# Differential attention: the head norm in three sets of tokens, spread over the next key projection, and two output projections begun inside the last head norm

## The reference, cut to what matters

```python
def _diff_attend(q, k, v, lam):
    s = jnp.einsum('bqhte,bkhte->bhtqk', q, k).astype(jnp.float32) * (q.shape[-1] ** -0.5)
    p = jax.nn.softmax(s, axis=-1)
    a = (p[:, :, 0] - lam * p[:, :, 1]).astype(v.dtype)
    return jnp.einsum('bhqk,bkhe->bqhe', a, v)
...
    yb = _sweep_query_blocks(lambda n, qn: _diff_attend(qn, kb_all, vb_all, lam), qb)
    yb = rmsnorm(yb, b_subln_g) * (1.0 - lam_init)
    y = jnp.concatenate([ya.reshape(B, S, -1), yb.reshape(B, S, -1)], axis=-1) * jax.nn.silu(g)
    x = x + gate * (y @ w_out)
```

## Time and profile before

| | |
|---|---|
| runs | 3954.23, 3945.95, 3941.73 us; median 3945.95 us |
| span of the profiled execution (first to last instruction) | 3950.5 us; the profile gives no other time for this execution |
| mean granted TensorE clock | 0.942 of full speed |
| PE busy | 3589.2 us, 91% of the span |
| PEld busy | 2836.7 us, 72% |
| DVE busy | 1908.9 us, 48% |
| ACT busy | 1348.4 us, 34% |
| POOL busy | 237.2 us, 6% |
| differential attention, heads 0 to 3 | about 2310 to 2820 us, then the last head norm until 2838 us |

### The profile page before, as it was taken

The page is one execution under the profiler, slowest core; times in us unless marked ns, Lnnn a source line. Parts: engine busy times, 40 slices in busy tenths (PEclk is TensorE's granted clock), DMA queues, the critical chain, the costliest instruction groups (busy, mean ns, idle before and its releaser), DMA issues. The chain is left out here.

```text
span 3950.5 us, 44451 instructions
## 1 busy us (share of the span) xinstructions
PE 3589.2 (91%) x18426; PEld 2836.7 (72%) x18426; DVE 1908.9 (48%) x3579; ACT 1348.4 (34%) x2445; POOL 237.2 (6%) x342
## 2 busy tenths in 40 slices
PE   7999989997989999999999988888798998888888
PEld 5888867664777888888766577777686665676676
DVE  4599952443834323322566644445345444224443
ACT  3211253544212211111322334444324555324441
POOL 1011110000100000000000000000000000000000
PEclk9699998998999999999999998988798999889999
DMA  3223321000521111111201011000221000000112
GB/s 113 91 100 119 128 107 55 29 22 36 204 96 32 49 51 56 48 43 46 99 29 35 24 34 34 27 29 23 105 74 53 32 32 26 27 24 16 34 50 84
DMA packets 69289, 228.90 MB, mean 58 GB/s; under 512 B 8728, under 2 KB 12824, under 8 KB 69088
## 3 DMA queue, kind: packets, MB, share of 16 engines
q1 hardware_dynamic: 43056, 132.68, 10.2%
q0 software_dynamic: 22576, 80.80, 6.0%
q10 hardware_dynamic: 3456, 12.58, 0.8%
HBM read 179.37 MB, written 36.17 MB: 55 GB/s over the span
## 5 line engine op out<-in xcount | busy, mean ns | idle before, releaser
L2421 PE MATMUL PS<-m,m 128*128 128x512 f32 (+3 forms) x3560 | 1426.3, 402 | 96.0 <-DVE m L2767 18.8
L2423 PE MATMUL PS<-m,m 128*128 128x512 f32 (+3 forms) x3560 | 1368.5, 386 | 0.0
L2422 PE MATMUL PS<-m,m 128*128 128x512 f32 (+3 forms) x3560 | 1366.9, 385 | 0.0
L2421 PEld LDWEIGHTS PS<-m,m 128*128 128x128 f32 (+2 forms) x3560 | 681.1, 192 | 300.1 <-issue 43.6
L2423 PEld LDWEIGHTS PS<-m,m 128*128 128x128 f32 (+2 forms) x3560 | 681.3, 192 | 135.6 <-issue 1.6
L2422 PEld LDWEIGHTS PS<-m,m 128*128 128x128 f32 (+2 forms) x3560 | 684.7, 193 | 120.2 <-issue 2.3
L2767 DVE TENSOR_TENSOR m<-m,m 128x1024 fp32r<-128x1024 f32 (+5 forms) x204 | 210.7, 1033 | 423.9 <-ACT m L2609 422.9
L2701 ACT COPY m<-PS 128x512 f32<-128x512 f32 x352 | 205.4, 589 | 458.1 <-PE PS L2528 457.4
L2538 PE MATMUL PS<-m,m 128*64 128x256 f32 (+1 forms) x1408 | 310.4, 413 | 28.4 <-ACT m L2701 21.2
L2519 PE MATMUL PS<-m,m 64*128 64x256 f32 (+5 forms) x1968 | 253.6, 369 | 62.5 <-ACT m L2690 43.5
L2519 PEld LDWEIGHTS PS<-m,m 64*128 64x128 f32 (+1 forms) x1968 | 214.5, 198 | 111.3 <-ACT m L2690 54.3
(11 more groups left out here) (190 smaller groups left out, 3037.1 us busy)
## 6 DMA issues: line engine op xcount, KB each, us to landing
m<-in_w SPq DMA_DIRECT2D x220, 512.0 KB, 3.3
g_scratch<-m ACTq DMA_DIRECT2D x24, 512.0 KB, 2.6
m<-g_scratch POOLq DMA_DIRECT2D x24, 512.0 KB, 4.7
m<-in_w SPq DMA_DIRECT2D x32, 256.0 KB, 2.6
x_scratch<-m POOLq DMA_DIRECT2D x2, 4096.0 KB, 13.5
m<-m POOLq DMA_DIRECT2D x60, 128.0 KB, 2.7
m<-in_xT POOLq DMA_DIRECT2D x24, 256.0 KB, 7.8
y_scratch<-m POOLq DMA_DIRECT2D x12, 512.0 KB, 2.9
```

The costliest lines, as they stand in the source:

```text
L2421: pe.e.engine.matmul(o, L[0], X[0], start=start, stop=False)
L2422: pe.e.engine.matmul(o, L[0], X[1], start=False, stop=False)
L2423: return pe.e.engine.matmul(o, L[1], X[0], start=False, stop=stop)
```

## The change

- In heads 1 and 2 the order of the fill becomes: squares of the head norm, transposes of v, then the k projection with the rest of the head norm put between its sets of tokens, then q, then v. `cols` and `root` are done for each of the three sets of tokens by themselves (16, 16 and 8 single-column hardware matmuls), and their `rows` and `subln` follow one set of the k projection later. The weights of k are therefore loaded before those of q, for all heads.
- In head 3's fill the norm of head 2 stays in one piece, but it too goes by three sets.
- After head 3, seven k-steps of the first set of `eo0` and seven of `eo1` are put between the three sets of the last head norm; their eighth k-step (k = 7) follows once the result is split. `cols` and `rows` there take turns on banks 6 and 7.
- The counts given to `Fill` and `head` change from (87, 87, 87, 63) and (11, 11, 11, 11) to (79, 85, 85, 62) and (3, 24, 24, 10).

The diff:

```diff
-            tiles += [(f"f{s}{h + 1}", 8, 128) for s in "qkv"]
+            tiles += [(f"f{s}{h + 1}", 8, 128) for s in "kqv"]
...
+            if last and "settled" in u:
+                assert u["settled"]()
...
-        def next_steps(chunks, nxt, banks):
+        def next_steps(chunks, nxt, banks, free=()):
...
-                    e_ = copy_to(lambda t0, tn: z[:, t0:t0 + tn], scale)
+                    e_ = copy_to(lambda t0, tn: z[:, t0:t0 + tn], scale, after=free)
...
             def finish_steps(h, free, banks):
                 p.add("gsilu", n=h, z=zg[:, :], after=gate_done)
+                squared = []
                 for t0, tn in CH2:
-                    n = p.id()
-                    p.add("square", n=n, x=yt[:, t0:t0 + tn], q=zq[:, t0:t0 + tn], r=None, after=list(free))
+                    squared.append((S.square, p.id()))
+                    p.add("square", n=p.n, x=yt[:, t0:t0 + tn], q=zq[:, t0:t0 + tn], r=None, after=list(free))
                     yield
-                of = roots(take(banks), [[(zq[:, 128 * y:128 * y + 128], cc("o128")[:, 0:1]), (ident, squares[h % 2][:, y:y + 1])]
-                                         for y in range(10)], [(S.square, n), squares_done[h]], eps=False, at_=inverse)
+
+                def roots_of(c):
+                    t0, tn = CH2[c]
+                    return roots(take(banks), [[(zq[:, 128 * y:128 * y + 128], cc("o128")[:, 0:1]), (ident, squares[h % 2][:, y:y + 1])]
+                                               for y in range(t0 // 128, (t0 + tn) // 128)], [squared[c], squares_done[h]], eps=False,
+                                 at_=inverse[:, t0 // 128:(t0 + tn) // 128])
+                of = roots_of(0)
                 yield
                 for c, (t0, tn) in enumerate(CH2):
                     b = take(banks)
-                    r, t = spread(b, of, t0 // 128, tn)
+                    r, t = spread(b, of, 0, tn)
...
-                    yield
+                    if c < 2:
+                        of = roots_of(c + 1)
+                        yield
...
+                settled_heads.append(h)
+                yield
...
                 def steps():
+                    old = finish_steps(h - 1, ready, at.fill_banks) if h else iter(())
                     if h:
-                        yield from finish_steps(h - 1, ready, at.fill_banks)
+                        for _ in range(3):
+                            next(old)
+                            yield
+                    if h == 3:
+                        yield from old
                     yield from token_major_steps(zv, 10, [(vt, None, 0, 0, 128)], ev["v"], at.fill_banks, at.v_after)
                     if h < 3:
-                        qk, v = ({s: x for s, x in nxt.items() if s in of} for of in ("qk", "v"))
-                        yield from next_steps(CHE, qk, at.fill_banks)
+                        q, k, v = ({s: x for s, x in nxt.items() if s == of} for of in "qkv")
+                        if h:
+                            next(old)
+                        yield from weave(next_steps(CHE, k, at.fill_banks, list(begin + rest)), old, 8)
+                        yield from next_steps(CHE, q, at.fill_banks)
                         yield from weave(next_steps(CHE, v, at.fill_banks), rotate_steps(nxt, done), 2)
...
-                at.run(units, list(begin), Fill(steps(), 11 + (76 if h < 3 else 52)), 11, tail,
+                at.run(units, list(begin), Fill(steps(), (3, 9, 9, 10)[h] + (76 if h < 3 else 52)), (3, 24, 24, 10)[h], tail,
...
-            for _ in finish_steps(3, ready, None):
-                pass
+            eo_evac = {}
+            eo = [linear_steps(f"eo{d}", h_rhs, CH2[0:1] + CH2[2:3] + CH2[1:2], lambda *a, d=d: eo_evac[d](*a), ahead=2 - d)
+                  for d in range(2)]
+            old = finish_steps(3, ready, [6, 7])
+            for n, of in zip((0, 0, 0, 4, 3, 7), (0, 0, 0, 0, 0, 1)):
+                next(old)
+                for _ in range(n):
+                    next(eo[of])
+            finish(old)
...
+        for d in range(2):
+            eo_evac[d] = add_gated(d, sums)
+            finish(eo[d])
+            if d == 0:
+                w_prep(st["use"] + 1)
+        two_sets([(f"eo{d}", h_rhs, add_gated(d, sums)) for d in range(2, 8)], CH2[0:1] + CH2[2:3], CH2[1:2],
```

More of the change, by code:

```diff
@@ L2001, in schedule @@
             p.add("gain8", out=g8[:, :], g=vc("subln"))
-            stored, squares_done = [], {}
+            stored, squares_done, settled_heads = [], {}, []
             def load_steps():
@@ L2081, in schedule @@
                                   "keys": [(128 * y, vt[:, k0 // 128 + y, :]) for y in range(n // 128)],
+                                  "settled": lambda h=h: len(settled_heads) >= h,
                                   "evac": (yt[:, 128 * b0:128 * b0 + 256], slice(0, P), None, y_free)})
                 units[0]["hook"] = functools.partial(p.add, "ready", on="pe", after=list(rest))
-                at.run(units, list(begin), Fill(steps(), 11 + (76 if h < 3 else 52)), 11, tail,
+                at.run(units, list(begin), Fill(steps(), (3, 9, 9, 10)[h] + (76 if h < 3 else 52)), (3, 24, 24, 10)[h], tail,
                        Fill(gate_steps(f"eg{4 + h}", CH2, done, at.tail_banks), 24) if h < 3 else None)
@@ L2110, in schedule @@
         sums = Squares(bufs[1], bufs[0])
-        two_sets([(f"eo{d}", h_rhs, add_gated(d, sums)) for d in range(8)], CH2[0:1] + CH2[2:3], CH2[1:2],
+        for d in range(2):
[4 more added lines that the diff above has]
+        two_sets([(f"eo{d}", h_rhs, add_gated(d, sums)) for d in range(2, 8)], CH2[0:1] + CH2[2:3], CH2[1:2],
                    modulated("od", bufs, sums, [0, 2]))
```

## The result

The changed kernel takes 3970.58 us (median of 4 runs, 3964.43 to 3973.69), the one before 3946.40 (4 runs): ratio 1.0056, interval 1.0042 to 1.0070. It is slower by 24 us by the medians, by 22 by the ratio, and outside the range that was forecast.

What follows compares the result with a forecast made beforehand. TensorE was taken to bound the kernel, losing to waits and half clock in heads 1 and 2. Terms 2 × 1.1 + 0.9 − 1.5 + 2.4 = +4.0 us on 3945.95 gave about 3950 us, range 3936 to 3960.

Steps and rivals of the forecast that it cites:

- What comes: waits: Heads 1 and 2, each: new TensorE waits of 1.9, 0.7, 2.5 and 2.3, sum 7.4 us, 2.6 more than before.
- the sum for heads 1 and 2: Heads 1 and 2, each: +2.6 for waits − 1.5 for clock = +1.1 us, between about −4.5 and +5.
- the copy was waited for before too and is not counted: Heads 1 and 2: ScalarE's copy at each set's end, 0.7 us, left out because it was already waited for.
- What comes: clock: Heads 1 and 2, each: half-clock surcharge 4.3 us first, 1.7 in later groups; sum 6.0, 1.5 less than before.
- falls in every group: Rival, heads 1 and 2 and last norm: projections run at half clock, +6 us per head, about 3966 us; chance 0.11.
- Head 3's fill: Norm of head 2 in head 3's stage: more root and `subln` waits, 0.9 us later; bounds −1 and +3.
- Head 0's stage: Stage without a norm: smaller share per pair leaves fill for the last pairs, 1.5 us gained; bounds −3 and 0.
- The last norm: After head 3: +0.7 us from the exposed wait for the split, +2.4 with half clock; bounds −1 and +6.
- The loads of x cost nothing: After the last norm: x loads move 6 us later, costed at nothing, at most 2 us, as TensorE has six banks.
- The table drain: Rival, heads 1 and 2: first root 2.8 us later in each through drains at table switches, about 3955 us; chance 0.03.

Runs made afterwards that it cites:

- set ends last: Kernel before, with head 2's norm by sets in head 3's fill, and ten early steps, estimate 82, in heads 1 and 2: 3929.69 us, ratio 0.9945.
- that and the tail: "set ends last" plus last norm by sets, seven early steps of each output projection, third projection's weights ahead of the late addition: 3928.82 us, 0.9947 to kernel before.

## Why the prediction was wrong, step by step

- **What comes: waits** was right for what it looked at. Forecast 1.9, 0.7, 2.5 and 2 × 1.15; measured 1.78, 0.69, 2.53 (3.19 in head 2) and 2 × 1.10. The first pair of head 1 became 5.6 us shorter (22.7 to 17.1). The second became 14.6 us longer (9.9 to 24.5), with 21 more projection matmuls (45 instead of 24, 4.8 us at 0.23 each) and the rest of the norm in it.
- The step that failed is the sum for heads 1 and 2, +1.1 each, measured +11.6 and +11.1: it has no term for the waits in the later pairs. It stopped at the last step of the norm. For head 0 I did ask what a smaller share per pair does, for heads 1 and 2 not, although the 24 early steps and the estimate of 85 were in the diff. The order of the later pairs would have shown a set's copy right ahead of the exponentials in five of them: at 1.5 to 2.4 us each, 8.7 us of waits where there had been 2.9. And "the copy was waited for before too and is not counted" holds only as long as the copies keep their places.
- **What comes: clock.** First stretch 13.7 us (forecast 12 to 14), then 3.4 and 6.8 us; I had taken half of 3.4 us of surcharge for the later ones. (The 3.4 us are 17 projections at 0.2 us, which is one group; for both groups the upper end had to be 6.8.) The half-clock time came to 3.4 us more than before, where the forecast had less. All of the busy time that head 1 gained is 2.2 us, so the rival "falls in every group", whose time of 3966 us was the nearest, was near for the wrong reason: it asked for 6 us of clock per head.
- **Head 3's fill**: forecast +0.9, measured −5.3. Idle time fell by only 1.8 us (32.3 to 30.5); the rest is clock, 0.82 instead of 0.78, and unchanged code reached 0.83 once, so how much is the change's is open. I priced waits there and left the clock out, which moves this stage by more.
- **Head 0's stage**: forecast −1.5, measured 0.0: TensorE's idle time fell by 0.8 us and its busy time rose by as much.
- **The last norm**: forecast +2.4, measured +4.3. The wait for the split was right (3.85). That tail took +2.4 to +7.0 over unchanged code, by which profiles are compared. "The loads of x cost nothing" was wrong: I looked for TensorE's banks, not for what stands behind the late addition in the lists of ScalarE and VectorE. Putting that right gave 2.6 us.
- The table drain of about 1.4 us in the Trainium skill, "ScalarE: Activation LUTs", section "What ACT_TABLE_LOAD costs", was weighed and left out of the sum. After, the exponential behind a load that begins at 2426.64 starts at 2427.93, 1.29 us later, and the root wait came out at 2.53 us as computed without a drain. So the trace doesn't agree with that section:

```profile
2426.64 1.28 ACT L2723 ACT_TABLE_LOAD   x1
2426.67 3.48 PEld L2490 LDWEIGHTS PS<-m,m 128*128 128x128 f32 x16 [0.88 <-ACT m L2685]
2426.67 3.57 PE L2490 MATMUL PS<-m,m 128*128 128x1 f32 x16 [0.47 <-ACT m L2685]
2427.93 1.11 ACT L2723 ACTIVATE m<-PS,m 128x1024 f32<-128x1024 f32 x1
```

## What to carry to other kernels

When filler work is dealt out in equal shares, and a share is as long as its own period, its end falls on one place in every round; look where that is in each engine's list, put it behind the work that the next round waits for, and count again whenever an offset changes. On an engine with an in-order list, an instruction that waits for a late input stops what stands behind it on that engine, and on others that need that; so read both lists, not the busier one. And price a shift of filler over the whole stage, not only where the new work stands.

## What the runs showed that I had not expected

Two steps of a fill, 1.4 us of work, moved a stage of some 135 us by 10 to 13 us, in both orders. And head 0, with the same instructions in the same order, took 120.8 to 120.9 us in some profiles and 123.6 to 124.5 in seven others; in these TensorE was idle no longer but spent about 13 us at half clock instead of 3. Head 1 has the same code in "set ends last" and "that and the tail" and took 131.0 and 133.7 us, with 20.5 and 27.3 us at half clock. A gain of 3 or 4 us in a single stage of a single profile is therefore no evidence by itself, that of head 3 included.
